# A two-layer attention and SwiGLU kernel: order, tables and products of the second attention, banks of the down products, and the last rows

## What is computed

```python
for l in range(DEPTH):                       # DEPTH = 2
    h = _modulate(_layernorm(x), sh1, sc1)   # and hc for the context
    y, yc = _token_mixers(h, hc, ...)        # a: _gqa; b: _neighbourhood_attn; c: _fourier_mix
    x = _layernorm(DEEPNORM_ALPHA * x + g1 * y, ln1_g[l], ln1_b[l])
    f = _swiglu(_modulate(_layernorm(x), sh2, sc2), w_gu[l], w_down[l])
    x = _layernorm(DEEPNORM_ALPHA * x + g2 * f, ln2_g[l], ln2_b[l])

# attention of either kind, per head
p = jax.nn.softmax(s + bias, axis=-1)        # keys: latent ones (b: a window) and all context
o = jnp.einsum('bhqs,bshd->bqhd', p, v)

# the merge
ga, gb, gf = jnp.split(jax.nn.sigmoid(gz), N_BRANCH, axis=-1)
y = (ga * (oa @ w_branch[0]) + gb * (ob @ w_branch[1]) + gf * (oc @ w_branch[2])) @ w_out
```

## Time and profile before

| | |
|---|---|
| median of 3 runs | 2324.91 us (2324.25 to 2325.17) |
| the profiled execution | 2324.89 us, of which the span of its instructions 2323.1 us |
| instructions | 34464, of them 13050 matmuls |
| mean granted TensorE clock | 0.996 of full speed |
| busy share | PE 97%, PEld 89%, DVE 51%, POOL 48%, ACT 40% |
| chain that ended last | PE 81%, DVE 10%, ACT 4%, issue 2%, POOL 1%, DMA 1% |
| HBM | 254.68 MB read, 10.49 MB written |

### The profile page before, as it was taken

How to read it: one execution, slowest core, us unless ns; L and a number is a source line. 1 busy time by engine, 2 the same in 40 slices (tenths; PEclk the granted TensorE clock), 3 DMA queues, 4 the chain that set the end, 5 groups by cost and what they waited for, 6 DMA issues and landing times.

```text
span 2323.1 us, 34464 instructions
## 1 busy us (share of the span) xinstructions
PE 2253.0 (97%) x13050; PEld 2061.9 (89%) x13050; DVE 1196.4 (51%) x2441; ACT 940.4 (40%) x1878; POOL 1107.4 (48%) x868
## 2 busy tenths in 40 slices
PE   7999999999999999999999999999999999999997
PEld 4899988989999999999998888888889889888887
DVE  6979766527732546654832364656637436112114
ACT  4231466436632651111112364356546547222223
POOL 1434455435534553433534563446545567545555
PEclk9999999999999999999999999999999999999999
DMA  6634200122214445443523453211223255323334
GB/s 267 226 109 145 83 28 28 55 71 75 65 60 136 159 153 192 135 154 112 161 90 118 154 165 121 73 55 37 70 85 96 77 187 190 119 95 102 112 124 169
DMA packets 122388, 270.23 MB, mean 116 GB/s; under 512 B 13956, under 2 KB 14212, under 8 KB 120840
## 3 DMA queue, kind: packets, MB, share of 16 engines
q1 hardware_dynamic: 113312, 245.43, 32.4%
q10 hardware_dynamic: 8936, 22.95, 2.8%
HBM read 254.68 MB, written 10.49 MB: 114 GB/s over the span
## 4 chain that ended last, share of the span: by engine, by line
PE 81%; DVE 10%; ACT 4%; issue 2%; POOL 1%; DMA 1%; ACTq 0%; SPq 0%; DVEq 0%
PE ps L2024 31%; PE ps L2036 12%; PE ps L2026 12%; PE ps L2434 7%; PE ps L2137 7%; PE ps L2404 4%; PE ps L2386 2%; PE ps L2367 2%; DVE pt_lo L1730 1%; PE ps L2213 1%; POOL w_lo L621 1%; DVE ada_unused_gate_up L1260 1%; DVE max_c L1713 1%; DMA raw<-in_stream 1%; DVE ada_unused_merge_c L1260 1%
## 5 line engine op out<-in xcount | busy, mean ns | idle before, releaser
L621 POOL TENSOR_TENSOR w_lo<-raw,w_hi 128x512 fp32r<-128x512 f32 x648 | 887.5, 1392 | 924.8 <-ACT w_hi L699 924.4
L699 ACT ACTIVATE w_hi<-raw 128x512 fp32r<-128x512 f32 x648 | 376.9, 626 | 666.9 <-PE ps L2026 213.0
L2024 PE MATMUL ps<-h_hi,w_lo 128*128 128x512 f32 (+1 forms) x832 | 304.6, 366 | 0.0
L2024 PE MATMUL ps<-h_hi,w_hi 128*128 128x512 f32 (+1 forms) x832 | 303.9, 365 | 0.0
L2024 PE MATMUL ps<-h_lo,w_hi 128*128 128x512 f32 (+1 forms) x832 | 303.9, 365 | 0.0
L633 POOL TENSOR_TENSOR p_sb<-p_sb,row_inv 128x768 f32<-128x768 f32 (+1 forms) x160 | 179.0, 1126 | 205.4 <-DVE row_inv L1723 203.8
L1828 DVE TENSOR_TENSOR ps<-silu_g,ps 128x512 f32<-128x512 f32 (+3 forms) x52 | 36.7, 705 | 354.9 <-PE ps L2024 191.1
L2024 PEld LDWEIGHTS ps<-h_hi,w_hi 128*128 128x128 f32 x832 | 156.2, 188 | 18.6
L2024 PEld LDWEIGHTS ps<-h_hi,w_lo 128*128 128x128 f32 x832 | 156.2, 188 | 18.3
L2024 PEld LDWEIGHTS ps<-h_lo,w_hi 128*128 128x128 f32 x832 | 156.2, 188 | 18.2
L2434 PE MATMUL ps<-h_hi,w_lo 128*128 128x384 f32 (+1 forms) x408 | 147.8, 362 | 1.0 <-ACT gates_a L1024 0.7
(11 more groups left out here) (246 smaller groups left out, 5461.4 us busy)
## 6 DMA issues: line engine op xcount, KB each, us to landing
raw<-in_stream SPq DMA_DIRECT2D x648, 256.0 KB, 2.9
ada_raw_gate_up<-in_w_ada SPq DMA_DIRECT2D x48, 512.0 KB, 3.5
ada_raw_tokens_a<-in_w_ada SPq DMA_DIRECT2D x16, 512.0 KB, 5.3
ada_raw_merge_c<-in_w_ada SPq DMA_DIRECT2D x16, 512.0 KB, 3.6
bias_sb<-in_bias ACTq DMA_DIRECT2D x32, 256.0 KB, 2.7
scratch<-xr ACTq DMA_DIRECT2D x16, 512.0 KB, 4.7
xr<-scratch SPq DMA_DIRECT2D x14, 512.0 KB, 4.9
first_raw<-in_w_first SPq DMA_DIRECT2D x5, 1024.0 KB, 14.2
```

Of the source, the lines that this page charges most:

```text
L621: nc.gpsimd.tensor_tensor(w_lo[:, u % 2, cols], raw[:, u % 2, cols], w_hi[:, u % 2, cols].bitcast(F32), ALU.subtract).then_inc(S("lo_made" ...
L699: nc.scalar.activation(w_hi[:, s, cols], raw[:, s, cols], ACT.Copy).then_inc(S("hi_made"), 1)
L2024: last = nc.tensor.matmul(bank(0), tile, x[:, k, 0:split], start=start, stop=stop)
```

## The change

**Second attention, products.** pt_hi and pt_lo become the two halves of one buffer. `attend` first waits for hi_out of each group and makes the high products of the shared key tiles, then for lo_out and makes the low products; this holds for part 0 too. A lone key tile's high and low parts go through one product of 256 columns, which writes two blocks of 128 columns, 256 columns apart in the bank. VectorE adds the second half of the bank to o_sum in `fold_low` (64x256, 32 times); `folded` is raised by that in those slots. In part 1 the outputs of slots alternate between banks 2 and 5, and `attend` waits for the fold of a slot earlier.

**Second attention, order.** In VectorE's `late_slot` both low copies stand behind `fill_rest`, with `fold_low(n - 1)` ahead of it. The key copies are issued by ScalarE's queue behind `key_parts`.

**Tables.** The sigmoid's `load_table` is gone. The exponential's stands at the start of both attentions instead of merge_c and `values`.

**Down.** The loop takes four units, with banks 0, 2, 4, 6 by turns, and waits for `summed` of the unit four before; `gate_up` begins with less strict waits for the last sums.

**Tail.** In the last group each tile's mean stands right behind its add; the last tile's shift and store are done in two halves of 512 columns.

```diff
-TURN_BANK, OUT_BANK, FILL_BANK = (4, 3), (6, 5), (7, 6)
+TURN_BANK, OUT_BANKS, FILL_BANK = (4, 3), ((6, 6), (2, 5)), (7, 6)
+DOWN_BANKS = 4
...
+def last_rows(ph, g):
+
+    return ph.kind == "bridge" and ph.part == 1 and ph.layer == DEPTH - 1 and g == len(ph.groups) - 1
...
+    pt = [sb(f"pt{b}", [P, 2, pt_n[b]], F32R, at=R + (69, 93)[b] * K) for b in range(2)]
+    pt_hi, pt_lo = ([pt[b][:, part, :] for b in range(2)] for part in range(2))
...
+                    if last_rows(ph, g) and i == len(ph.groups[g]) - 1:
+                        act.dma_start(out[t, :, 0:LAT], xr[:, t, 0:LAT]).then_inc(S("stored"), 16)
+                        act.wait_ge(S("shifted"), at(ph, "shifted") + len(ph.groups[0]) * g + i + 2)
+                        act.dma_start(out[t, :, LAT:D], xr[:, t, LAT:D]).then_inc(S("stored"), 16)
+                        continue
...
+            def key_copies(c, filled):
+
+                act.wait_ge(S("fill_out"), filled)
+                for x in range(2):
+                    n = 2 * (c % 2) + x
+                    act.dma_start(k_hh[1][HD * (1 - x):HD * (2 - x), n, :].bitcast(F32), k_hh[1][HD * x:HD * x + HD, n, :].bitcast(F32)).then_inc(S("k_dup"), 16)
...
             def values(ph):
                 act.wait_ge(S("merged"), at(ph, "merged"))
-                load_table(ACT.Exp)
...
                 unit_done(ph.unit, 0, lambda: key_parts(0, qk_bank(0, 1), 0, TOK))
+                key_copies(0, at(ph, "fill_out") + 1)
...
                             act.wait_ge(S("ada_used"), PRIME - ADA_FIRST + ADA_WINDOWS[ph.kind][1])
-                        load_table(ACT.Exp)
...
                         fill_out(f, len(fill_passes(ph, f)) - 1)
+                        if f < 6 and f % 2:
+                            key_copies(f // 2 + 1, at(ph, "fill_out") + passes_to(ph, f + 1))
...
-                    if n == count - 2:
-                        load_table(ACT.Sigmoid)
...
+                load_table(ACT.Exp)
                 act.wait_ge(S("merged"), at(ph, "merged"))
                 probs(0, 0)
...
-                    if i:
+                    if last_rows(ph, g):
+                        tile_mean(i)
+                    elif i:
                         tile_mean(i - 1)
...
+                    if last_rows(ph, g) and i == n - 1:
+                        for half in range(2):
+                            cols = slice(LAT * half, LAT * (half + 1))
+                            nc.vector.scalar_tensor_tensor(xr[:, t, cols], scaled[:, cols], inv_s[:, t:t + 1], ln_rows[:, 1, cols],
+                                                           ALU.mult, ALU.add).then_inc(S("shifted"), 1)
+                        return
...
+                def fold_low(n):
+
+                    h, j = divmod(n, pairs)
+                    if branch == 0 or j == 2:
+                        return
+                    rows = slice(HD * (h % 2), HD * (h % 2) + HD)
+                    dve.wait_ge(S("part_folded"), at(ph, "part_folded") + 2 * h + j + 1)
+                    nc.vector.tensor_tensor(o_sum[1][rows, j, :], ps[0:HD, out_at(1, n)[0], 2 * P:4 * P], o_sum[1][rows, j, :], ALU.add
                                             ).then_inc(S("folded"), 1)
...
-                    turned_lo(n, 0)
+                    if n:
+                        fold_low(n - 1)
                     if late is not None:
                         fill_rest(late, 0)
...
-                    for g in groups[1:]:
+                    for g in groups:
                         turned_lo(n, g)
...
+                    for s in range(DOWN_BANKS):
+                        n = DOWN_BANKS * i + s
+                        if s % 2 and ada:
+                            ada_three("gate_up", (beside[0] + ADA_SLOTS * (n // 2)) // ADA_SLOTS)
                         dve.wait_ge(S("unit_done"), ph.unit + n + 1)
...
+                    def product_of(g, kt, part, start=False):
+
+                        a = 512 * g + turn_col(branch, j, g, kt, min(ORDER[branch][j], key=lambda t: t % 2))
+                        return nc.tensor.matmul(ps[:, bank, out_col:out_col + 2 * P], value(kt), pt[branch][:, part, a:a + 2 * P],
+                                                start=start, stop=part == 1 and g == len(groups) - 1, skip_group_check=True)
+
+                    def lone_product(g, kt, t):
+
+                        a, col = 512 * g + turn_col(branch, j, g, kt, t), P * (t % 2)
+                        return nc.tensor.matmul(ps[:, bank, :].rearrange("p (a b) -> p a b", a=2)[:, :, col:col + P], value(kt),
+                                                pt[branch][:, :, a:a + P], start=False, stop=True, skip_group_check=True)
+
                     for g in some:
                         if g == 0:
-                            wait(pe, "folded", at(ph, "folded") + n)
+                            wait(pe, "folded", at(ph, "folded") + n - branch)
+                        pe.wait_ge(S("hi_out"), at(ph, "hi_out") + turns["p", n, g] + 1)
+                        for kt in groups[g]:
+                            if len(users_of(kt)) == 2:
+                                product_of(g, kt, 0, start=g == 0 and kt == groups[0][0])
+                    for g in some:
                         pe.wait_ge(S("lo_out"), at(ph, "lo_out") + turns["p", n, g] + 1)
...
+                        for kt in groups[g]:
+                            users = users_of(kt)
+                            last = product_of(g, kt, 1) if len(users) == 2 else lone_product(g, kt, users[0])
...
-                with pe.Fori(0, KD // 2) as i:
-                    for s in range(2):
-                        pe.wait_ge(S("summed"), at(ph, "summed") + 2 * i + s - 1)
...
+                with pe.Fori(0, KD // DOWN_BANKS) as i:
+                    for s in range(DOWN_BANKS):
+                        pe.wait_ge(S("summed"), at(ph, "summed") + DOWN_BANKS * i + s - DOWN_BANKS + 1)
```

More of the change, by code:

```diff
@@ L505, in load_cond @@
                              ).then_inc(S("cond_loaded"), 16)
-            def key_copies(ph, u):
-                if ph.kind == "values" and u == ph.unit + 4:
-                    c, filled = 0, at(ph, "fill_out") + 1
-                elif ph.kind == "attention" and ph.part and u - ph.unit in (5, 7, 9):
-                    f = u - ph.unit - 4
-                    c, filled = f // 2 + 1, at(ph, "fill_out") + passes_to(ph, f + 1)
-                else:
-                    return
-                sp.wait_ge(S("fill_out"), filled)
-                for x in range(2):
-                    n = 2 * (c % 2) + x
-                    sp.dma_start(k_hh[1][HD * (1 - x):HD * (2 - x), n, :].bitcast(F32), k_hh[1][HD * x:HD * x + HD, n, :].bitcast(F32)
-                                 ).then_inc(S("k_dup"), 16)
             def rows_of(ph, t):
@@ L1003, in move_half @@
                         act.wait_ge(S("folded"), at(ph, "folded") + n - 1)
-                    nc.scalar.activation(o_half[branch][rows, n % 2, :], ps[other, OUT_BANK[branch], a:a + 2 * P], ACT.Copy).then_inc(S("moved"), 1)
+                    nc.scalar.activation(o_half[branch][rows, n % 2, :], ps[other, bank, a:a + 2 * P], ACT.Copy).then_inc(S("moved"), 1)
                 def out_hi(n):
@@ L1104, in attention @@
                         split(ph.unit + f + 2, f % 2)
+                        if branch == 1 and f < 6 and f % 2:
+                            key_copies(f // 2 + 1, at(ph, "fill_out") + passes_to(ph, f + 1))
                     h, j = divmod(n, pairs)
@@ L1358, in tile_mean @@
                 def tile_mean(i):
+                    if ends(ph):
+                        return
                     dve.wait_ge(S("shifted"), at(ph, "shifted") + base + i + 1)
-                    if not ends(ph):
-                        mean(ph, 1, tiles[i])
+                    mean(ph, 1, tiles[i])
                 for i in range(n - 1):
@@ L1735, in fold @@
                     h, j = divmod(n, pairs)
-                    a, rows = 2 * P * (n % 2), slice(HD * (h % 2), HD * (h % 2) + HD)
+                    (bank, a), rows = out_at(branch, n), slice(HD * (h % 2), HD * (h % 2) + HD)
                     dve.wait_ge(S("moved"), at(ph, "moved") + n + 1)
@@ L1739, in fold @@
                         dve.wait_ge(S("o_lo"), at(ph, "o_lo") + pairs * (h // 2 - 1) + j + 1)
-                    nc.vector.tensor_tensor(o_sum[branch][rows, j, :], ps[rows, OUT_BANK[branch], a:a + 2 * P], o_half[branch][rows, n % 2, :], ALU.add
+                    nc.vector.tensor_tensor(o_sum[branch][rows, j, :], ps[rows, bank, a:a + 2 * P], o_half[branch][rows, n % 2, :], ALU.add
+                                            ).then_inc(S("part_folded" if branch and j < 2 else "folded"), 1)
+                def fold_low(n):
+                    h, j = divmod(n, pairs)
+                    if branch == 0 or j == 2:
+                        return
+                    rows = slice(HD * (h % 2), HD * (h % 2) + HD)
```

(16 more changed lines are left out.)

48 lines of the change are left out of this document (19 added, 29 removed).

## The result

The changed kernel took 2300.39 us (median of 4 runs, 2299.30 to 2301.04) beside 2325.04 us before on the same chip: 24.65 us less, a ratio of 0.9891 with a 95% interval of 0.9874 to 0.9908. In a later comparison it was 2299.00 beside 2326.57, 0.9883 (0.9867 to 0.9900). The span went from 2323.1 to 2298.2 us, 24.9 less. The forecast was 2303.9 with 2298 to 2312.

A forecast was written before the change was run, and what follows sets the result against it. TensorE, busy 97% of a 2323.1 us span, was taken as the bound. Terms summed to 22.3 us, less 1.3 for returning stalls: 2324.9 - 21.0 = 2303.9 us, range 2298 to 2312.

The forecast's parts named there:

- six score waits on the key remainder: Second attention, three per layer: TensorE's score waits of 0.88 us each were to vanish from the profile after.
- Key copies: Two per pass, eight times, moved from SP's queue to ScalarE's idle 0.67 us: taken as 0, bound eight times 0.5.
- The rival that bundled it with the tables: Table loads don't fit their new places and key copies hinder ScalarE: 6.4 us back, 2310.3 us; chance 0.08.
- Order of VectorE: Second attention: key remainder done before TensorE asks, ending three score stalls per layer, 6 x 0.88 = 5.3 us.
- Lone key tiles: Second attention: two products of 256 columns replace four of 128, 0.15 us in 26 slots, 3.9 us.
- The slower rival: Two-block product in PSUM runs as two products with a gap; at 0.5 us each 2332 us; chance 0.03.
- High products first: Second attention: high products fill waits for low copies; 1.6 + 1.3 us in part 1, 1.2 in part 0.
- Tables: Moved table loads end TensorE waits at the ends of parts and in merge_c: 3.3 + 1.0 + 1.4 us.
- Clock: Layer 0, behind part 0's end: with 0.2 us of wait left, no fall to 1.2 GHz; 1.6 us.
- Down: Layer 0's second part: four banks end the sum waits, but POOL's low weights come next; 0.5 us, bounds 0 and 3.8.
- Tail: Kernel's end: earlier means and the last store in halves, together 1.2 us, bounds 0.6 and 1.8.
- the deduction of 1.3: Taken off the summed 22.3 us because a stall ended in one slot of part 1 partly returns in the next.

The follow-up runs named there:

- e1: The changed kernel with the key copies issued by SyncE's queue again, as before the change; 2297.11 us.
- e9: The changed kernel with key copies on SyncE's queue, lone products apart, no half-sums, and the first low copy ahead of the remainders as before; 2310.45 us.
- e4: The changed kernel with key copies on SyncE's queue and lone key tiles' high and low parts as two products, without the added half-sums; 2303.19 us.
- e5: The changed kernel with a slot's first low copy ahead of the half-sum and the remainders again; 2311.75 us.
- e6: The changed kernel, but value products wait for a group's low copy before its first product, as before; 2301.73 us.
- e3: The changed kernel with the table loads back at their places of before; 2304.48 us.
- e10: The changed kernel with table loads at their old places and value products that wait for the low copy first; 2309.46 us.
- e2: The changed kernel with two banks by turns in down instead of four, gate_up's waits as before the change; 2301.07 us.

## Why the prediction was right, and where its terms were wrong

- **Bound and direction**: right. TensorE's order bounds nearly everything, and the gain came where its waits and the columns taken off it were. 24.7 us against 21.0. Of the signs named, one failed: six score waits on the key remainder stand.
- **Key copies**: wrong, and by most. The term was 0, set against a ScalarE "which then is idle for 0.67 us". Issuing two copies takes 1.1 to 2.2 us. The trace of before has that duration in SyncE's queue (1.07 us, once 1.73), and it was not held against the idle time of the queue that got them. It cost 4.2 us (e1). The rival that bundled it with the tables priced it at 3.2; its table half did not happen, so the rival as a whole did not come.
- **Order of VectorE**: the mechanism was right for the scores, the size too small. The step that failed is "the last low copy ends no sooner, as VectorE is busy without a gap there": there was a gap, the wait for the high copy ahead of the first low copy (0.33 us there, a mean of 0.69 in layer 0), and the remainder now fills it. Layer 0's value waits shrank by the order itself, from 4.2 us in e9 to 0.3 in e4. The order was worth 8.4 us (e9 against e4); the forecast had 5.3 for the scores, and put all of the 2.9 of the value waits down to other parts. The 5.3 came only with the copies moved back.
- **Lone key tiles**: right in mechanism, the size too small: 0.2 a slot for 0.15, and in all 32 slots, 6.1 us for 3.9. The shorter step behind the products was left out, and six slots were left out for the stalls behind them, which then vanished. The half-sums lay in idle time in the new order. In the old one they did not quite (e5's three value waits), which the term-by-term sum didn't say. The slower rival, two blocks at twice the cost, did not happen. Its arithmetic was off too: by the forecast's own terms a product of 0.5 us gives 2328 and not 2332, and the change breaks even at 0.45 and not 0.39.
- **High products first**: too large in sum, 3.0 us (e6) for 1.2 + 2.9 = 4.1, and misplaced: 2.5 in part 0 and not 1.2, and 0.5 in part 1 and not 2.9.
- **Tables**: 4.9 (e3) beside forecast 3.3 + 1.0 + 1.4 = 5.7. With high products first, the table's waits are partly filled; each was priced as if alone. No load at its new place was late. Each took 1.28 us, and where ScalarE had work at hand the next activation started 1.29 us after the load. The Trainium skill (ScalarE: Activation LUTs, What ACT_TABLE_LOAD costs) gives about 2.66 us for a switch, a load and a drain; the traces disagree, and the waits of up to 0.9 us estimated from it did not come.
- **Clock**: right, 1.6 of merge_a's 3.2 us. The reason given, that less wait is left, is borne out by e10, where the wait and the fall came back. That the high products alone kept the clock (e3) was not foreseen, and rests on two broken waits. Why an equal wait at times brings no fall stays open.
- **Down**: the mechanism was right (low weights next). The banks are worth 0.7 for 0.5; the phase gained 1.8, with 1.1 unexplained.
- **Tail**: right, 1.5 for 1.2.
- **Sum**: the deduction of 1.3 for stalls that return was not needed; the missed 4.2 of the copies was covered by what the order (3.1) and the lone tiles (2.2) brought above their terms. The range held, but errors of 4 and 5 us cancelled, which is luck. The range's lower end is not what its terms give either: with down and part 0 at their bounds the sum is 2300.1 and not 2298, and 2300.39 was measured.

## What to carry to other kernels

When a transfer's issue is moved to a queue of an engine that computes, set the issue's duration, not the number of issues, against that engine's gap, and look at what stands behind it: an idle time put down to another engine can be the queue's own issuing. In an in-order engine put first the work that waits for nothing, and let the copies that wait for another engine follow together. Try edits in pairs as well as alone: here the new adds were free in the new order and brought value waits in the old one, and tables and product order cost more undone together than apart. To size parts of a few microseconds, compare phases between profiles: the start of this kernel alone differed by up to 3.8 us between profiled executions.

## What the runs showed of the hardware

- A key copy's issue on ScalarE's or SyncE's queue took 0.47 to 1.70 us, where a bias load's took 0.33 to 0.46. Ten of the fourteen traces have one over 0.61 us, in the last key pass of layer 1, or in e2 in the first of its part 1; e4, e5, e9 and e10 have none.
- At the end of part 0 an unbroken wait of TensorE of 1.77 to 1.83 us was followed in three of four cases by 3.4 us at 1.2 GHz; the same wait with two products in it (1.09 and 0.23) was not. In merge_c of e4 a wait of 1.83 us was followed by one too, and a wait of 1.94 us in a bridge of e2 was not.
- A product of 256 columns that writes two separate blocks of 128 took 0.12 us by starts, as a contiguous one.
